# Six late expert groups form their rows on TensorE, one result buffer, and part of a gate projection moved into the attention heads

## The reference

```python
h = rmsnorm(x, norm1_w) * (1 + sc1) + sh1
(u_in, gate_b, gate_c, q, k, v, g_out, lr_f, lr_b, gate_br_conv, gate_br_gla) = split(h @ w_in)
y_gla = gla_mixer(...)                       # 4 heads, forward and backward scan over chunks of 64
merged = sigmoid(gate_br_conv) * (y_conv @ w_br_conv) + sigmoid(gate_br_gla) * (y_gla @ w_br_gla)
x = x + g1 * (merged @ w_out)
h2 = rmsnorm(x, norm2_w) * (1 + sc2) + sh2
# moe: 64 experts of width 256, the best 8 of each token by sigmoid scores, and one shared expert
act = silu(t @ w_gate[e]) * (t @ w_up[e]) * weight[t, e];  routed = sum_e act @ w_down[e]
x = x + g2 * (routed + shared);  y = rmsnorm(x, final_norm_w)
```

## Time and profile before

| | |
|---|---|
| three runs | 1000.52, 1003.54, 1006.48 us, median 1003.54 |
| profiled execution | 1000.46 us, its span 998.7 us |
| PE busy | 913.7 us (91%) |
| DVE, ACT, POOL busy | 438.2, 187.9, 104.6 us |
| DMA | 324.24 MB, mean 325 GB/s |
| granted TensorE clock, mean | 0.977 |

### The profile page before, as it was taken

One profiled execution on the slowest core, in us unless ns is written; L12 is line 12 of the kernel. 1 busy time (PEld: TensorE's weight loads), 2 busy tenths in 40 slices (PEclk: granted clock), 3 DMA queues, 4 the chain that ended last, 5 costly groups with the idle time before them and its releaser, 6 DMA issues.

```text
span 998.7 us, 12909 instructions
## 1 busy us (share of the span) xinstructions
PE 913.7 (91%) x4821; PEld 476.4 (48%) x4821; DVE 438.2 (44%) x761; ACT 187.9 (19%) x289; POOL 104.6 (10%) x210
## 2 busy tenths in 40 slices
PE   4999999989999999899999999988979897988795
PEld 0455567675555588544444444433434343433332
DVE  3229866569542343624344333332332232332257
ACT  2140501111000002212222212121121111221111
POOL 3000000000000000101222111220221121211100
PEclk9999999999999999999999999998999999998898
DMA  9932463407558298989999999999999999999995
GB/s 374 290 117 84 150 229 129 167 1 260 204 186 319 91 375 335 384 358 403 368 370 421 420 420 420 420 420 421 419 420 422 419 421 419 420 421 420 422 419 229
DMA packets 82816, 324.24 MB, mean 325 GB/s; under 512 B 10398, under 2 KB 39242, under 8 KB 52800
## 3 DMA queue, kind: packets, MB, share of 16 engines
q1 hardware_dynamic: 67296, 289.43, 72.7%
q0 software_dynamic: 10080, 24.44, 6.3%
q10 hardware_dynamic: 5376, 9.52, 2.7%
HBM read 301.52 MB, written 34.11 MB: 336 GB/s over the span
## 4 chain that ended last, share of the span: by engine, by line
PE 82%; DVE 5%; DMA 5%; issue 5%; ACT 2%; SPq 0%; DVEq 0%
PE bank L573 26%; PE bank L1791 21%; PE bank L602 13%; PE bank L1963 4%; PE bank L1950 4%; DMA arena<-expert_rows 3%; DMA arena<-in_w_mod_dram 2%; PE bank L560 2%; PE bank L1990 2%; PE bank L1865 2%; ACT arena L584 1%; PE bank L591 1%; DVE arena L587 1%; PE bank L533 1%; PE bank L2051 1%
## 5 line engine op out<-in xcount | busy, mean ns | idle before, releaser
L573 PE MATMUL bank<-arena 128*32 128x512 f32 (+2 forms) x1536 | 267.8, 616 | 33.8 <-issue 32.5
L1791 PE MATMUL bank<-arena 128*128 128x384 f32 x640 | 208.0, 487 | 0.0
L573 PEld LDWEIGHTS bank<-arena 128*32 128x32 f32 (+2 forms) x1536 | 94.0, 128 | 204.7 <-issue 204.7
L1791 PEld LDWEIGHTS bank<-arena 128*128 128x128 f32 x640 | 121.3, 190 | 86.1 <-issue 2.6
L602 PE MATMUL bank<-arena 128*32 128x512 f32 (+2 forms) x768 | 131.5, 595 | 5.9 <-issue 5.2
L602 PEld LDWEIGHTS bank<-arena 128*32 128x32 f32 (+2 forms) x768 | 44.5, 123 | 70.3 <-issue 70.3
L430 DVE SCALAR_TENSOR_TENSOR arena<-arena 128x2048 f32<-128x2048 f32 x28 | 64.6, 2349 | 28.4 <-DMA arena<-in_w_mod_dram 27.4
L607 DVE SCALAR_TENSOR_TENSOR arena<-bank,arena 128x512 f32<-128x512 f32 x36 | 27.0, 751 | 109.2 <-PE bank L602 109.1
L615 ACT ACTIVATE arena<-arena 128x1024 f32<-128x1024 f32 x36 | 41.4, 1151 | 166.2 <-DVE arena L611 163.6
L587 DVE TENSOR_TENSOR arena<-arena,bank 128x256 f32<-128x256 f32 x36 | 21.8, 605 | 113.5 <-ACT arena L584 113.5
L547 POOL DMA_INDIRECT arena<-h_rows,arena x36 | 38.3, 1064 | 239.6 <-issue 123.1
(11 more groups left out here) (254 smaller groups left out, 735.9 us busy)
## 6 DMA issues: line engine op xcount, KB each, us to landing
arena<-in_w_gate_e_dram SPq DMA_DIRECT2D x64, 1024.0 KB, 26.8
arena<-in_w_up_e_dram SPq DMA_DIRECT2D x64, 1024.0 KB, 29.2
arena<-in_w_down_e_dram SPq DMA_DIRECT2D x64, 1024.0 KB, 29.3
arena<-in_w_mod_dram SPq DMA_DIRECT2D x24, 1024.0 KB, 7.3
arena<-in_w_in_dram SPq DMA_DIRECT2D x22, 1024.0 KB, 6.0
expert_rows<-arena SPq DMA_DIRECT2D x6, 2048.0 KB, 23.5
arena<-expert_rows SPq DMA_DIRECT2D x12, 1024.0 KB, 25.8
arena<-in_w_out_dram SPq DMA_DIRECT2D x4, 1024.0 KB, 5.6
```

The costliest lines, as they stand in the source:

```text
L573: ins = pe.matmul(bank[off:off + width, :], x_T[:, k, off:off + width], w[:, :, k, :], start=(k == 0), stop=(k == KT - 1))
L1791: ins = pe.matmul(ps[:, 0:TOK], w[:, k, P * (n % 2):P * (n % 2) + P], hT[:, k, :], start=(k == 0), stop=(k == KT - 1))
```

## The change

- Four of the eight tiles of `gbc` (its first four) are computed inside the heads: half a tile (4 matmuls) ahead of the intra-chunk output, half behind it. ACT applies their sigmoid there. The `w_mod` units are loaded behind other units.
- The two fixed experts become groups of two (96 rows beside 32 of rank 63 or 62) and the first two groups; four more groups of two follow. Still 36 groups, 28 with two experts and 8 with one, but the eight come at groups 6, 9, 13, 17, 21, 24, 28 and 32 (before: 1, 3, 5, 10, 15, 20, 25 and 30).
- Groups 15, 19, 23, 27, 31 and 34 (`ON_CHIP`) gather nothing: PE forms their rows, already transposed, as products of the normed tokens `h2`, which stay in SBUF, with the one-hot matrices: 24 matmuls of 128x128 in place of 8 transposes.
- Both entries of `y_e` are one buffer, so DVE waits for the scatter of group `i-1` before it writes the results of group `i`. The gate rows move to the freed buffer, since `h2` must stay.
- The shared result is folded into `x1` by DVE right behind group 0's gate and up, straight from the banks; ACT no longer copies it.
- Groups 0 to 34 are scattered (`ADDED = NQ - 1`), only the last is added on PE; PE also adds piece 6, and pieces 4, 5 and 6 share one semaphore.

```diff
-    fixed = [[(r, 0, 128)] for r in range(FIXED)]
+    fixed = [wide_and_narrow(i, i, NE - 1 - i) for i in range(FIXED)]
-    first = [pairs.pop(0), fixed[0], pairs.pop(0), fixed[1], pairs.pop(0)]
+    first = fixed + [pairs.pop(0) for i in range(4)]
...
+ON_CHIP = [15, 19, 23, 27, 31, 34]
-ADDED = NQ - 2
-ON_PE = [[], [4, 5], [8, 9]]
+ADDED = NQ - 1
+ON_PE = [[], [4, 5, 6], [8, 9]]
...
-        y_e = [at(a, D) for a in (a_x + 2 * D, a_x + 3 * D)]
+        y_e = [at(a_x + 2 * D, D)] * 2
...
-        together = [(0, 1), (2, 3), (4, 5), (6, 7), (8, 9), (10,), (11,)]
+        together = [(0, 1), (2, 3), (4, 5, 6), (7,), (8, 9), (10,), (11,)]
...
+        def rows_from_tokens(pe, b, part):
+            for k in part:
+                for t in range(NT):
+                    ins = pe.matmul(banks[k // 4][:, P * (k % 4):P * (k % 4) + P], h2[:, t, P * k:P * k + P],
+                                    onehot[b][:, t, :], start=(t == 0), stop=(t == NT - 1))
+            return ins
...
             def gather(i):
+                if i in ON_CHIP:
+                    return
...
+                if i in ON_CHIP:
+                    pe.wait_ge(x["onehot_done"], i + 1)
+                    ins = rows_from_tokens(pe, i % 2, range(4 * part, 4 * part + 4))
+                else:
+                    ins = rows_to_features(pe, i % 2, range(4 * part, 4 * part + 4))
...
                 silu_product(dve, banks[2 + i % 2]).then_inc(x["act_done"], 1)
+                if i == 0:
+                    fold_shared()
...
-                if i >= 2:
-                    dve.wait_ge(x["scattered"][i % 2], 16 * (i // 2))
+                if i:
+                    dve.wait_ge(x["scattered"][(i - 1) % 2], 16 * ((i + 1) // 2))
...
+                project_part("gbc", h, 0, 4)
                 job = ("o", h)
...
+                project_part("gbc", h, 4, KT)
                 for d in range(2):
                     if d and h + 1 < NH:
                         chunk_scores(h + 1)
...
-            project("gbc", KT)
+            project("gbc", KT, NH)
...
-            add_group(pe, 0, 2)
-            add_group(pe, 1, 0, True).then_inc(S["low_summed"], 1)
-            for t in range(1, NT):
-                add_group(pe, 1, t)
-            for t in range(1, NT):
+            for t in range(NT):
+                ins = add_last_group(pe, t)
                 for n in ON_PE[t]:
                     ins = add_piece(pe, n, n == ON_PE[t][-1])
                 ins.then_inc(S["low_summed"], 1)
```

More of the change, by code:

```diff
@@ L138, in plan_jobs @@
     jobs += [("ss", NH - 1)]
-    jobs += [("gbc", n) for n in range(KT)]
+    jobs += [("gbc", n) for n in range(NH, KT)]
     jobs += [("gbg", n) for n in range(6)] + [("mod", 2)] + [("gbg", n) for n in range(6, KT)]
@@ L624, in sp_experts @@
             sp.wait_ge(S["order_ready"], 1)
-            first, second, third = [[r for r, off, width in quad] for quad in QUADS if quad[0][0] >= FIXED][:3]
+            first = [r for quad in QUADS[:FIXED] for r, off, width in quad if r >= FIXED]
+            second, third = [[r for r, off, width in quad] for quad in QUADS[FIXED:FIXED + 2]]
             def number(r):
@@ L632, in sp_experts @@
                 load_gate_up(sp, x, e, slot_of[r])
-            for r, e in zip(first, ids):
                 load_down(sp, x, e, slot_of[r])
@@ L854, in end_gate, with fold_shared @@
                 gate_of_sample(dve, i % 4).then_inc(x["gate_done"], 1)
[L856 to L860 removed]
+            def fold_shared():
+                for t in range(NT):
+                    for n in range(2):
+                        job, part = ("sy", t, n), slice(512 * n, 512 * n + 512)
+                        full(dve, job)
+                        ins = dve.tensor_tensor(folded, bank(job)[:, :], g2_rows[:, SEQ_OF[t], part], ALU.mult)
+                        free(ins, job)
+                        drained(dve, job)
+                        link(dve.tensor_tensor(x1[:, t, part], x1[:, t, part], folded, ALU.add))
                 dve.sem_inc(S["tile_folded"], 1)
@@ L956, in pe_spill @@
                 down(pe, whole).then_inc(x["y_done"], 1)
-            pe.wait_ge(x["y_b"], NE * (c + 1))
-            for t in range(2):
-                add_group(pe, 0, t)
             rows_are_in(pe, c + 2)
@@ L1637, in _, with gate @@
                     free(act.activation(k_tail[:, d, h, :], bank(("kt", d, h))[:, 0:TOK], ACT.Copy), ("kt", d, h))
+            def gate(name, dst, tiles=range(KT)):
+                for n in tiles:
+                    full(act, (name, n))
+                    free(act.activation(dst[:, n, :], bank((name, n))[:, 0:TOK], ACT.Sigmoid), (name, n))
             for h in range(NH):
+                gate("gbc", g_conv, [h])
                 full(act, ("o", h))
@@ L1653, in _ @@
             act.dma_start(new_state[0, 0].rearrange("w h k v -> k (w h) v"), new_st).then_inc(S["out_done"], 16)
-            def gate(name, dst, tiles=range(KT)):
-                for n in tiles:
-                    full(act, (name, n))
-                    free(act.activation(dst[:, n, :], bank((name, n))[:, 0:TOK], ACT.Sigmoid), (name, n))
-            gate("gbc", g_conv)
+            gate("gbc", g_conv, range(NH, KT))
             gate("gbg", g_gla, range(KT - 1))
@@ L1723, in _ @@
             act_x_half(act, X[0], 0)
-            def shared_out():
-                act.wait_ge(S["h2_out"], 16 * NT)
-                for t in range(NT):
-                    for i in range(2):
-                        job = ("sy", t, i)
-                        full(act, job)
-                        free(act.activation(y_shared[:, t, 512 * i:512 * i + 512], bank(job)[:, :], ACT.Copy), job)
-            act_experts(act, X[0], shared_out)
+            act_experts(act, X[0])
             act.dma_start(last_w, final_norm_w.unsqueeze(0).to_broadcast([P, D])).then_inc(S["norm_w_in"], 16)
```

87 lines of the change are left out of this document (39 added, 48 removed).

## The result

Median of the runs: 994.38 us for the changed kernel (990.31 to 995.23), 1004.28 us for the kernel before (1000.52 to 1006.48). The ratio is 0.989, with a 95% interval of 0.986 to 0.993. The change makes the kernel about 10 us faster. The prediction had 1001.6 us and "the same" as the likeliest case; its range ended at 994.8. In the profiled executions the span falls from 998.7 to 988.6.

What follows compares the result with a forecast made beforehand. PE bounds the first half and first 16 groups, transfers what follows, then a chain at the end. An earlier loop, fuller transfers and fewer gathers, less the costlier end, give span 996.8 against 998.7: 1003.54 - 1.9 = 1001.6 us, range 994.8 to 1007.

Steps and rivals of the forecast that it cites:

- the same: Whole kernel: time not told from no change, within about 0.5% (5 us), faster meaning below 998.5, slower above 1008.6.
- Heads: Projection tiles inside the heads fill 4.3 us of PE's waits for DVE; 1.0 is paid at the modulation.
- The wait at the modulation: PE's wait at the sum of the second modulation, its last unit being late: 0 to 2 us, taken as 1.
- First groups: Before the loop, POOL's extra pick and reversal for group 1 delay PE's second look-up: cost 1.4 us.
- The start of the loop: Group 0 on PE starts 4.3 - 1.0 - 1.4 = 1.9 us earlier.
- Transfers: Weight stream: idle slots filled from 445 to 515 save 7.2 us, six gathers fewer 5.0; last weights land at 941.2.
- Products: In the six groups without gathers, 24 products cost PE 5.6 us, net 4.3 more per group; group 34 ends at 935.0.
- One buffer: In the loop, DVE's wait for the previous scatter costs nothing: 10.5 us to its landing, 13.03 per group.
- The end: Behind the loop, reads wait for group 34's scatter until 945.5, DMA engines run dry; piece 6 at 966.5, span end 996.8.
- The rival with the emptier DMA engines: At the end, scatter in 6 us not 8.2, clock kept (2.6), modulation in time (1.0): 5.8 less, 995.8; chance 0.31.
- the slow start: PE's additions of pieces in the tail start at a lower clock after over 4 us of waiting: 2.6 us added.
- DVE's own chain: In the tail, DVE's additions reach the last sums about 986, before PE is done at 988.7, so they do not bind.

Runs made afterwards that it cites:

- the first repair: Changed kernel with pieces 4 and 5 on one semaphore, piece 6 on another, and the last group's three products ahead of all pieces: 989.13 us, ratio 0.984.

## Why the prediction was right or wrong

In the profiled executions the forecast span was 996.8 and the measured one 988.6, 8.2 less. The steps:

**Heads: mechanism right, size wrong, and this is the first of the two terms that failed.** Forecast 4.3 - 1.0 = 3.3 us earlier, measured 5.2 to 5.5. The listed waits (4.3) leave out the overlap of following work that each wait also destroys; from start to start it was 5.6. The wait at the modulation was 0.20, at the good end of the stated 0 to 2: its last unit was not late.

**First groups: cost 0.5 us, not 1.4.** The second look-up comes 2.05 us behind the first instead of 1.81. Of pick and reversal most lay beside other work.

**The start of the loop** is thus 4.9 us earlier by mechanisms, not 1.9. The other 3 of the measured 7.9 are lapses of the clock that the first profile before had twice and the first profile after not at all. With one lapse each, as in most profiles, 429.70 to 430.26 stands for the changed kernel and 434.83 for the kernel before (with the new end), 4.6 to 5.1 us apart.

**Transfers: both terms confirmed.** 408 and 421 GB/s where 415 was asked for; without the new order the windows fall by 6.2 us worth of transfers (forecast 7.2), without the products the last weights come about 4.7 us later at the same start (forecast 5.0). The last weights landed at 936.2, forecast 941.2, and that 5.0 is the loop's start (6.0 early) and 1.0 of loss.

**Products: the cost right, the conclusion wrong.** 5.55 to 5.78 us per group against 5.6. Group 30 at 856.87 to the end of group 34 at 929.75 are 72.9 us, forecast 73.8, so the working of this stretch held. But "the products use up most of what the gathers gave" did not: taking them away costs 5.4 us, all the gathers gave. The prediction compared PE's sum with the transfers' and added both where they met; it left out that without the products PE waits there and then runs at the lower clock (4.14 us, and 9.77 for 7.04), a price that stood in its own. This did not move the sum, which followed PE through the products in either case.

**One buffer:** no wait of DVE for a scatter appears in the loop. Right.

**The end: right that the change costs here, wrong in the scatter, the second term that failed.** Forecast 8.2 us for the scatter of group 34, measured 5.07. The reads started at 937.1 instead of 945.5: 5.3 from the earlier end of group 34, 3.1 from the scatter. The rival with the emptier DMA engines named this mechanism and gave it 2.2 us; of the 5.8 us that it asked for in all, the runs show 5.2 (3.1 in the scatter, 1.3 in the clock, 0.8 at the modulation). The numbers for it were in the forecast: scatter issued at 937.3, weights in at 941.2, so by the table above landed at 942, not 945.5. Piece 6 came 22.7 us behind the start of the reads (forecast 21.0; 1.5 of the difference lies between the first piece, at 942.0, and the third, at 949.7, where 6.2 us were counted, and why stays open), PE needed 20.6 us from there (forecast 22.2; the slow start cost 1.3, not 2.6), DVE 8.15 behind it (8.1). One path was misjudged: the forecast had DVE's own chain ready 2.7 us ahead of PE, and in the trace it is ready 0.15 us behind PE, and the first repair, with PE done at 978.74, found its limit in DVE at 980.63.

The Trainium skill (TensorE: Matmul & The Clock Gate, HAM oscillation — how this bites in real kernels) states that a wait for transfers lets the clock fall, so that the work behind it starts cold. The runs agree only in part. Over the loops of all the profiles here, gate and up took 8.3 to 10.0 us instead of 7.1 behind each of the 24 waits for weights of 3.8 to 5.1 us, behind 4 of the 6 of 3.2 to 3.8 (not behind 3.76 us in the kernel without products, nor behind 3.59 in the one with three), behind 8 of the 28 of 2.0 to 3.0, and behind none of the 45 shorter ones.

**The sum.** -8.4 us at the start of the reads, +1.7 until piece 6, -1.6 on PE: -8.3, and that is the miss. The first of these is the loop's start, 6.0 early (heads 1.3, modulation 0.8, second look-up 0.9, and 3.0 of lapses, which is the luck of one execution), and the scatter's 3.1, less 0.7 in the loop. Of the rivals the emptier DMA was nearest (995.8, medians 993.5 to 994.4). The three parts, each taken back alone, cost 6.7, 4.4 and 5.4 us, together 16.5, and the new end costs 5 to 8: that leaves 8 to 11 us, and the two ratios of the changed kernel say 9 to 11; without its end the change would be worth 17 (0.9826). The forecast of "same" came from a gain at the loop's start that was 3 us too small and a scatter that was 3 us too long, on top of an end that really cost.

What stays open: what sets the lapse of the clock near 383 in the kernel before, and differences of 2 to 3 us between the variants with three, nine and early products. The single result buffer and the new place of the shared result were not taken back alone; no wait of DVE or PE in the profiles points at either.

## What to carry to other kernels

Read the gain of filling a wait from start to start of the work around it, not from the listed waits: here 5.6 against 4.3 us. Where an engine waits for transfers anyway, work given to it that saves a transfer is free, and more than free while it keeps the clock up; put it in front of the waits, and stop when the waits are gone (six groups, not nine). Put too early it delays the moment when buffers come free, and with it the transfers (407 instead of 420 GB/s). Before the last weights land, something must already stand behind them in the queues: here the reads waited for the last scatter and the last of them landed 36.0 us behind the weights instead of 31.1, and that one edit took a third to a half of what the rest gave.

## What was not expected of the hardware

A scatter's time is mostly that of the transfers queued with it: 8.0 to 9.1 us among weights in the first profile of the changed kernel, 0.5 to 0.9 us behind the last weights where these end, 3.0 alone. The same program had a lapse of the granted clock of 1.7 us in one execution and not in the next, and waits of 2.0 to 3.0 us were followed by slow work 8 times out of 28. The kernel before, timed twice in one series, differed from itself by 2.2 us in the ratio.
